# First feed-forward product of a decoder layer: both halves of the normed rows moved as one stream of 512 columns

## The reference

```python
u = rms_norm(h, norm_mix)
z = u @ w_in
h = h + concat([rwkv7_time_mix(z[..., :RWKV_IN]), moba_attention(q, k, v)]) @ w_mix_out
h = h + memory_cross_attention(rms_norm(h, norm_xattn), rms_norm(mem, norm_mem), w_xq, w_xkv, w_xo)
a = square(relu(rms_norm(h, norm_ffn) @ w_ff1))      # 1024 -> 4096
h = h + a @ w_ff2                                    # 4096 -> 1024
out = rms_norm(h, norm_final)
```

## Time and profile before

| | us |
|---|---|
| median of 3 runs | 478.35 (477.77 to 478.5) |
| profiled execution, whole | 479.23 |
| its span, first to last instruction | 477.2 |
| TensorE busy | 459.2 |
| VectorE busy | 316.0 |
| ScalarE busy | 235.7 |
| mean granted TensorE clock | 0.994 |

### The profile page before, as it was taken

How to read it: one execution, slowest core, us unless ns; L and a number is a source line. 1 busy time by engine, 2 the same in 40 slices (tenths; PEclk the granted TensorE clock), 3 DMA queues, 4 the chain that set the end, 5 groups by cost and what they waited for, 6 DMA issues and landing times.

```text
span 477.2 us, 11032 instructions
## 1 busy us (share of the span) xinstructions
PE 459.2 (96%) x4774; PEld 429.8 (90%) x4774; DVE 316.0 (66%) x459; ACT 235.7 (49%) x357; POOL 34.8 (7%) x50
## 2 busy tenths in 40 slices
PE   4999999999999999999999997999999999999994
PEld 4999999989898899999998997989898989898983
DVE  4688999897576459668656486555466555554646
ACT  5779843343354235335543453544374555453534
POOL 8100000000000000151000053000000000000000
PEclk9999999999999999999999998999999999999998
DMA  7963534505060523554452363756555555756602
GB/s 256 332 218 102 177 105 159 182 10 172 3 203 15 166 89 99 168 177 142 133 166 89 94 181 97 232 169 198 178 178 177 177 181 178 233 195 205 197 2 88
DMA packets 61411, 73.09 MB, mean 153 GB/s; under 512 B 1314, under 2 KB 51572, under 8 KB 61364
## 3 DMA queue, kind: packets, MB, share of 16 engines
q1 hardware_dynamic: 61284, 72.14, 47.3%
q0 software_dynamic: 80, 0.26, 0.1%
HBM read 71.35 MB, written 1.05 MB: 152 GB/s over the span
## 4 chain that ended last, share of the span: by engine, by line
PE 90%; DVE 5%; issue 1%; DMA 1%; ACT 1%; SPq 0%; ACTq 0%; DVEq 0%
PE bank L482 17%; PE bank L483 16%; PE bank L484 16%; PE bank L499 6%; PE bank L500 6%; PE bank L501 6%; PE bank L449 2%; PE bank L450 2%; PE bank L451 2%; PE bank L851 2%; DMA xval<-in_x 1%; PE bank L875 1%; PE bank L611 1%; DVE w_lo L1543 1%; PE bank L777 1%
## 5 line engine op out<-in xcount | busy, mean ns | idle before, releaser
L1543 DVE TENSOR_TENSOR w_lo<-raw,w_hi 128x1024 fp32r<-128x1024 f32 x130 | 160.3, 1242 | 84.2 <-ACT w_hi L1051 84.0
L1051 ACT ACTIVATE w_hi<-raw 128x1024 fp32r<-128x1024 f32 x130 | 136.6, 1057 | 140.0 <-PE bank L484 80.1
L482 PE MATMUL bank<-op_hi,w_hi 128*128 128x256 f32 x672 | 195.1, 290 | 3.8 <-DVE w_lo L1543 3.0
L483 PE MATMUL bank<-op_lo,w_hi 128*128 128x256 f32 x672 | 190.7, 284 | 0.4 <-issue 0.4
L484 PE MATMUL bank<-op_hi,w_lo 128*128 128x256 f32 x672 | 190.7, 284 | 0.0
L482 PEld LDWEIGHTS bank<-op_hi,w_hi 128*128 128x128 f32 x672 | 129.4, 192 | 6.7 <-issue 4.6
L483 PEld LDWEIGHTS bank<-op_lo,w_hi 128*128 128x128 f32 x672 | 129.5, 193 | 0.5
L484 PEld LDWEIGHTS bank<-op_hi,w_lo 128*128 128x128 f32 x672 | 129.4, 193 | 0.4 <-issue 0.4
L499 PE MATMUL bank<-w_hi,op_hi 128*128 128x512 f32 x128 | 49.9, 390 | 0.0
L500 PE MATMUL bank<-w_lo,op_hi 128*128 128x512 f32 x128 | 49.9, 390 | 0.0
L501 PE MATMUL bank<-w_hi,op_lo 128*128 128x512 f32 x128 | 49.8, 389 | 0.0
(11 more groups left out here) (247 smaller groups left out, 487.1 us busy)
## 6 DMA issues: line engine op xcount, KB each, us to landing
raw<-in_w_ff SPq DMA_DIRECT2D x32, 1024.0 KB, 5.4
raw<-in_w_in SPq DMA_DIRECT2D x12, 1024.0 KB, 5.5
raw<-in_w_xkv SPq DMA_DIRECT2D x8, 1024.0 KB, 5.7
raw<-in_w_mix_out SPq DMA_DIRECT2D x4, 1024.0 KB, 5.0
raw<-in_w_xq SPq DMA_DIRECT2D x4, 1024.0 KB, 5.1
raw<-in_w_xo SPq DMA_DIRECT2D x4, 1024.0 KB, 5.7
xval<-in_x SPq DMA_DIRECT2D x2, 512.0 KB, 4.8
raw<-in_w_in SPq DMA_DIRECT2D x2, 512.0 KB, 5.7
```

The costliest lines, as they stand in the source:

```text
L482: mm(dst, wh[:, k, :], op_hi[which][:, k, :], start=first, stop=False)
L483: mm(dst, wh[:, k, :], op_lo[which][:, k, :], start=False, stop=False)
L1051: op(view(w_hi), r, ACT.Copy).then_inc(hi_done, 1)
L1543: tt(view(w_lo), r, view(w_hi).bitcast(f32), ALU.subtract).then_inc(lo_done, 1)
```

## The change

An `f1` half now moves the hi and the lo rows at once: the two operand tiles become one tile of [128, 2, 8, 256], and a step k is one matmul of 512 columns with w_hi, whose results land side by side (hi rows in columns 0 to 255, lo rows in columns 256 to 511), and one of 256 columns with w_lo, added to the first side. So a half fills a bank; the halves take the two banks in turn. ScalarE copies the second side into `tmp` (`part`), VectorE adds the first side to it (`add`), which frees the bank, and when both halves of a unit are there it takes relu and square in one instruction (`square`). ScalarE rounds the square (`hidden`), VectorE forms the lo part. The first `f1` unit no longer has its quarters mixed with those of the second one.

```diff
-    _late = {"mix": 0, "xo": 1, "f1": 1}.get(UNITS[_u][0])
+    _late = {"mix": 0, "xo": 1}.get(UNITS[_u][0])
...
-    elif _u == len(UNITS) - 1:
+    elif _u == len(UNITS) - 1 or UNITS[_u][0] == "f1" and UNITS[_u][4] == 0:
         QUARTERS += [(2 * _u + _i, _p) for _p in range(2) for _i in range(2)]
...
-        op_hi = [sb(f"op{i}_hi", [128, KT, T], f32r) for i in range(2)]
-        op_lo = [sb(f"op{i}_lo", [128, KT, T], f32r) for i in range(2)]
+        op_both = [sb("op0", [128, 2, KT, T], f32r), None]
+        op_hi = [op_both[0][:, 0, :, :], sb("op1_hi", [128, KT, T], f32r)]
+        op_lo = [op_both[0][:, 1, :, :], sb("op1_lo", [128, KT, T], f32r)]
...
+        def half_no(s):
+            return s - OUTS[FIRST["f1"]][1] if UNITS[s // 2][4] < 2 else 2 * UNITS[s // 2][4] + s % 2
+        def half_bank(s):
+            return dense_bank[(s + 1) % 2]
... (TensorE, quarter)
+                    if what == "f1":
+                        half = half_no(s)
+                        if half < 2:
+                            pe.wait_ge(out_taken, FIRST["f1"] - 1 + half)
+                        else:
+                            pe.wait_ge(dve_add, half - 1)
...
+                if what == "f1":
+                    b = half_bank(s)
+                    for k in range(4 * part, 4 * part + 4):
+                        first, final = q == BEGUN[s] and k % 4 == 0, q == DONE[s] and k % 4 == 3
+                        if opening and k % 2 == 0:
+                            pe.wait_ge(dve_op, op_no("xo", k // 2) + 1)
+                        if final:
+                            mm(b[:, 0:T], wl[:, k, :], op_hi[0][:, k, :], start=False, stop=False)
+                        last = mm(b[:, :], wh[:, k, :], op_both[0][:, :, k, :], start=first, stop=final)
+                        if not final:
+                            mm(b[:, 0:T], wl[:, k, :], op_hi[0][:, k, :], start=False, stop=False)
+                    if q == DONE[s]:
+                        last.then_inc(dense_mm, 1)
+                    return
... (ScalarE)
+            def part(n, half):
+                s = OUTS[FIRST["f1"] + n][1] + half
+                act.wait_ge(dense_mm, s + 1)
+                if n >= 2:
+                    act.wait_ge(dve_square, n - 1)
+                op(tmp[:, n % 2, T * half:T * half + T], half_bank(s)[:, T:2 * T], ACT.Copy).then_inc(act_part, 1)
             def hidden(o):
                 n = nth(o)
-                act.wait_ge(out_taken, o + 1)
+                act.wait_ge(dve_square, n + 1)
                 k = 4 * (n // 2 % 2) + 2 * (n % 2)
-                op(op_hi[1][:, k:k + 2, :], pair(tmp[:, n % 2, :]), ACT.Square).then_inc(act_hidden, 1)
+                op(op_hi[1][:, k:k + 2, :], pair(hid_sq[:, n % 2, :]), ACT.Copy).then_inc(act_hidden, 1)
-            def take(o):
-                ...
-                op(tmp[:, n % 2, :], dense_bank[o % 2][:, :], ACT.Relu).then_inc(out_taken, 1)
... (VectorE)
+            def add(n, half):
+                s = OUTS[FIRST["f1"] + n][1] + half
+                dve.wait_ge(act_part, 2 * n + half + 1)
+                x = tmp[:, n % 2, T * half:T * half + T]
+                tt(x, half_bank(s)[:, 0:T], x, ALU.add).then_inc(dve_add, 1)
+            def square(n):
+                dve.wait_ge(dve_add, 2 * n + 2)
+                if n >= 2:
+                    dve.wait_ge(dve_hidden, n - 1)
+                x = tmp[:, n % 2, :]
+                stt(out=hid_sq[:, n % 2, :], in0=x, scalar=0.0, in1=x, op0=ALU.max, op1=ALU.mult).then_inc(dve_square, 1)
             def hidden(n):
-                dve.wait_ge(out_taken, FIRST["f1"] + n + 1)
-                sq = hid_sq[:, n % 2, :]
-                link(tt(sq, tmp[:, n % 2, :], tmp[:, n % 2, :], ALU.mult))
                 dve.wait_ge(act_hidden, n + 1)
```

More of the change, by code:

```diff
@@ L1299, in _ @@
             hi(9)
-            follow(2)
+            load(1, 0)
             rates()
-            hi(10)
             key_sums()
             follow(3)
+            hi(10)
             hi(11)
@@ L1308, in _ @@
             hi(12)
+            hi(13)
             follow(4)
-            hi(13)
-            factor()
[L1312 to L1319, removed]
+            hi(14)
+            follow(5)
+            load(1, 1)
+            hi(15)
+            hi(16)
+            follow(6)
+            hi(17)
+            factor()
             hi(18)
-            tokens()
-            vtokens()
             hi(19)
@@ L1439, in _ @@
             hi(77)
+            part(3, 0)
             hi(78)
+            rms(3)
             hi(79)
+            follow(35)
             hi(80)
+            part(3, 1)
+            part(4, 0)
+            follow(36)
             hi(81)
-            take(36)
             hi(82)
-            follow(36)
+            part(4, 1)
+            part(5, 0)
             hi(83)
             hi(84)
+            follow(37)
+            part(5, 1)
             hi(85)
-            take(37)
             hi(86)
@@ L1482, in _ @@
             hi(103)
+            part(10, 0)
             hi(104)
             hi(105)
-            residual(2)
-            residual(3)
-            take(43)
-            follow(43)
             hi(106)
+            follow(42)
+            part(10, 1)
             hi(107)
-            take(44)
-            follow(44)
             hi(108)
@@ L1495, in _ @@
             hi(110)
+            part(11, 0)
+            follow(43)
             hi(111)
+            part(11, 1)
             hi(112)
+            part(12, 0)
+            follow(44)
             hi(113)
-            take(45)
-            follow(45)
+            part(12, 1)
             hi(114)
             hi(115)
-            take(46)
-            follow(46)
             hi(116)
+            part(13, 0)
+            follow(45)
+            part(13, 1)
             hi(117)
@@ L1510, in _ @@
             hi(121)
-            take(47)
-            follow(47)
+            part(14, 0)
+            follow(46)
+            part(14, 1)
             hi(122)
             hi(123)
-            take(48)
+            hi(124)
+            residual(3)
+            hi(125)
+            part(15, 0)
+            follow(47)
+            part(15, 1)
             follow(48)
-            hi(124)
-            hi(125)
             hi(126)
@@ L1978, in _ @@
             lo(9)
-            diagonal_of(1)
-            follow(2)
             take(3)
             sums()
-            follow(3)
-            spread_copy(1)
             key_norm()
             lo(10)
-            key_root()
+            sides()
+            load(1, 0)
+            follow(3)
             lo(11)
             take(4)
+            lo(12)
+            key_root()
+            follow(4)
+            take(5)
+            lo(13)
+            lo(14)
             keys(0)
+            lo(15)
@@ L1991, in _ @@
             keys(1)
-            lo(12)
-            follow(4)
-            lo(13)
-            take(5)
-            reads(0)
-            keys(2)
-            lo(14)
-            lo(15)
             follow(5)
             take(6)
+            follow(6)
             lo(16)
+            reads(0)
+            lo(17)
+            lo(18)
+            take(7)
+            load(1, 1)
+            keys(2)
+            lo(19)
+            take(8)
+            lo(20)
+            lo(21)
+            take(9)
@@ L2187, in _ @@
             lo(95)
+            add(7, 1)
+            square(7)
+            add(8, 0)
             lo(96)
             lo(97)
-            follow(41)
+            hidden(7)
+            add(8, 1)
+            square(8)
             lo(98)
             lo(99)
-            follow(42)
             lo(100)
+            add(9, 0)
             lo(101)
@@ L2197, in _ @@
             lo(103)
+            hidden(8)
+            add(9, 1)
+            square(9)
+            add(10, 0)
             lo(104)
             lo(105)
-            follow(43)
+            hidden(9)
+            add(10, 1)
             lo(106)
             lo(107)
-            follow(44)
             lo(108)
```

430 lines of the change are left out of this document (229 added, 201 removed).

## The result

The changed kernel takes 481.0 us (median of 5 runs, 480.1 to 482.5), the kernel before on the same chip 478.5. The medians lie 2.5 us apart; the ratio, taken over all runs, is 1.0062, with a 95% interval of 1.0044 to 1.0080, which is 3.0 us: slower by 0.6%, where 2.8 us faster was forecast and the range ended at 479.6. The two profiled executions show less of the difference: that of the changed kernel took 480.11 us, the lowest of its five, and that of before 479.23, above its median. Their spans are 478.3 and 477.2, 1.1 apart.

What follows compares the result with a forecast made beforehand. TensorE, with work for 96% of the span, was taken as the bound. Stream -3.4, xo to f1 -0.9, start +0.5 and mixer +1.0 took the profiled 479.23 to 476.4 us; for the median, 478.35 - 2.8 = 475.5 us, range 472.0 to 479.6.

Steps and rivals of the forecast that it cites:

- The mixer: Mixer jobs spread anew among the dense quarters: equal TensorE work, one more wait priced, +1.0 us, bounds -1.6 and +4.
- The stream: TensorE's f1 matmuls: a step falls from 0.360 to 0.3467 us over 256 steps, -3.4 us, bounds -3.4 and 0.
- Rival 1: f1 matmuls: the wide stream saves nothing, the operand's break costing 0.0133 us per instruction; 478.9 us, chance 0.14.
- From xo to f1: Change from last xo unit to f1: 4.6 us lost before becomes 3.7 in four pieces, -0.9 us, bounds -4.6 and +1.5.
- (a): From xo to f1: lo(65) stands behind follow(30) and take(31) on VectorE, so half 65 starts 0.9 us late.
- (b): From xo to f1: half 67 waits 0.65 us for the last xo unit's bank, which take(32) frees.
- (c): From xo to f1: last two k of half 66 wait 1.55 us for follow(32), 2.7 us long beside GpSimd.
- (d): From xo to f1: half 68 waits 0.6 us for the first add, which stands behind hi(69) and its copy.
- Banks, ScalarE and VectorE: In f1: banks come free in time and the engines' added work stays beside TensorE, so it costs nothing.
- rival 2: f1 banks come free late: 18 halves each wait 0.5 us, 484 us, or 0.3 us each, 481 us; chance 0.12.
- Rival 3: The mixer's new order waits at its upper bound: +3 more than taken, 478.5 us, up to 480; chance 0.14.
- rival 4: Waits at f1 mostly vanish, all but (c), and the mixer's two with them: -7.5, 471 us; chance 0.08.

Runs made afterwards that it cites:

- experiment 1: The changed kernel with the three lists of calls of the kernel before up to values(3): 474.4 us, ratio 0.9917 to the kernel before.
- experiment 2: The kernel before, its own f1 kept, with the changed kernel's lists of calls up to values(3): 484.7 us, ratio 1.0144 to the kernel before.
- experiment 7: The kernel of experiment 1 with the f1 operand laid out so 512 columns lie in one piece: 474.2 us, ratio 0.9918 to the kernel before.
- experiment 9: The kernel of experiment 1 with lo(68) put ahead of follow(32) in VectorE's list: 477.3 us, ratio 0.9982 to the kernel before.
- experiment 4: The changed kernel with one dense quarter moved between the two parts of the second join: 478.75 us, ratio 1.0007 to the kernel before.
- experiment 5: The changed kernel with SyncE holding the load of unit 17 until the second join ends: 480.2 us, ratio 1.0038 to the kernel before.
- experiment 6: The kernel of experiment 5 with the load held until the first four outq are done: 481.7 us, ratio 1.0075 to the kernel before.

## Why the prediction was wrong, step by step

*The mixer*, "one more wait of the size of the 0.9 us one: +1.0 us", is the step that failed. Measured are +6.6 to +6.9 us (experiments 1 and 2, by medians and by ratios), 5.7 of them up to `gate` and 0.9 behind it. I followed the lists for waits on engines and found small ones. They are there, but sum to some 2.0 us, twice the price: 1.4 for lo parts and 0.6 for ScalarE. The larger part, some 4.3 us, is one that I put at nothing: stops in which TensorE has no instructions (+2.7) and the lower clock behind the longest (+1.5 to 1.7). "TensorE's work is equal; only waits can change" was my ground, and I didn't ask whether its instructions arrive, though the diff puts 128 matmuls of 12 ns in a row and the reader can see SyncE's 1 MB loads between them. "The clock" was then priced at `f1` alone, and fell here. Even the bound of +4 was too near. The stop isn't the same in every execution: 2.40 us in the profiled, fastest one of the changed kernel, 2.97 in the profiled, slowest one of experiment 2. Why it varies stays open.

*The stream*, -3.4 us, was mis-sized: the right direction, -1.9. From the start of a 512 to that of its 256 it takes some 0.235 us, not 0.2267, and from there to the next 512 0.117, not 0.120; TensorE in order of time, changed kernel:

```profile
299.85 0.39 PE L495 MATMUL bank<-op,w_hi 128*128 128x512 f32 x1
300.08 0.28 PE L497 MATMUL bank<-op,w_lo 128*128 128x256 f32 x1
300.19 0.39 PE L495 MATMUL bank<-op,w_hi 128*128 128x512 f32 x1
300.43 0.28 PE L497 MATMUL bank<-op,w_lo 128*128 128x256 f32 x1
300.54 0.39 PE L495 MATMUL bank<-op,w_hi 128*128 128x512 f32 x1
```

A run of 32 steps went from 11.52 to 338.28 - 327.01 = 11.27 us, 0.352 per step for the 0.3467 forecast: (0.360 - 0.3525) x 256 = 1.9. Each spacing had been read in a stretch of equal widths; mixed, they don't add. Rival 1 (the break costs the 0.0133 us) is out by experiment 7; its sum by the Trainium skill's 2.5 ns per matmul (TensorE: Matmul & The Clock Gate, "Wait — 56ns, not 53.3ns?"), -0.6 us, is out by the 1.9 measured.

*From xo to f1*, -0.9 us, was too little: some -2.5. This is what is left of the 4.8 us that the changed kernel gains from the first `f1` half on, less the stream's 1.9 and the 0.3 us of piece (a), which falls ahead of it. (By the starts at the place itself it is -2.1: 4.6 before, 2.5 after, each with the slower first matmul behind a wait. The 4.6 came out in the prediction with the clock at 1.6 us; the starts give 1.4 for it and 3.2 for the wait.) The mechanism was right and all four pieces were mis-sized: (a) 0.3 us for 0.9, (b) 0.94 for 0.65, (c) 0.50 for 1.55, (d) nothing for 0.6. The clock stays at 1.00. Piece (c) is short mostly because `follow(32)` takes 1.92 us here, not 2.7; VectorE in order of time, changed kernel:

```profile
285.99 3.19 DVE L1585 TENSOR_TENSOR w_lo<-raw,w_hi 128x1024 fp32r<-128x1024 f32 x2
289.11 1.91 DVE L1646 SCALAR_TENSOR_TENSOR op<-hT,par,op 128x256 fp32r<-128x256 f32 x2
...
292.07 0.68 DVE L1605 TENSOR_TENSOR hT<-bank,hT 128x512 f32<-128x512 f32 x1
293.73 1.92 DVE L1646 SCALAR_TENSOR_TENSOR op<-hT,par,op 128x256 fp32r<-128x256 f32 x2 [0.98 <-ACT op L1101]
```

Experiment 9 shows that the place of `lo(68)` alone is worth 2.9 us, the clock included. The new order of the first quarters without the wide stream wasn't tried.

*Banks, ScalarE and VectorE*, 0, held. The waits list has no entry for an `add`. The groups after, from 290 to 472 us, stand near the costs taken (0.42, 0.39, 0.745, 0.63 us):

```profile
L1655 DVE TENSOR_TENSOR tmp<-bank,tmp 128x256 f32<-128x256 f32 x32 | 13.5, 421 | 21.5 <-ACT tmp L1110 21.5
L1110 ACT ACTIVATE tmp<-bank 128x256 f32<-128x256 f32 x32 | 11.9, 373 | 20.2 <-PE bank L495 20.2
L1663 DVE SCALAR_TENSOR_TENSOR s<-tmp 128x512 f32<-128x512 f32 x16 | 11.0, 690 | 0.4
...
L1117 ACT ACTIVATE op_hi<-s 128x512 fp32r<-128x512 f32 x16 | 10.0, 623 | 3.8 <-DVE s L1663 3.8
```

So rival 2 didn't happen. That its milder case, "with 0.3 us each: 481 us", gives the very time measured is chance. *The start*, +0.5, was -0.1 (17.94 to 17.82).

*The sum* by the profiled spans: -1.9 - 2.5 - 0.1 and +5.8 for the mixer (5.95 with the earlier start put back and piece (a) taken out) make +1.3, against +1.1. It closes nearly by construction, since two terms are differences of the same starts. Rival 3, the mixer's new order, had the right place, but waits on engines as its reason and +4 us at most for 6.6, and its 0.14 was too small; rival 4's low waits at `f1` came in part together with it. All three of my own signs of being wrong came true: the mixer's waits passed 4 us (they sum to over 6), the clock fell again, and a half is slower than 2.8 us, if barely (11.27 / 4 = 2.82). That the change wins 4.0 us without the mixer's new order doesn't make the forecast right, since it was for the kernel with that order.

## What to carry to other kernels

When calls are only moved, count instructions per microsecond on the engine, not its work: a row of short matmuls needs the next block of instructions early, and a big DMA beside it makes that late. Keep such bursts apart with long-running work between them, and away from the loads. The kernel before did both: three dense quarters stand between its two parts, and 57 and 4 GB/s were on the move beside them (105.9 to 107 and 111 to 113 us), so which of the two protects it was not separated. One quarter between them left stops of 1.30 and 0.55 us beside the load (experiment 4); holding the load left 0.49 and 0.22 at the join, but only moved the long stop (5 and 6). And when a change brings a new piece of work and new lists, price and time the two apart; here one was worth 4 us and the other cost nearly 7.

## What the runs showed of the hardware

- TensorE most likely ran out of instructions: the waits show only the word "issue", and the rest is the timing of the packets and experiments 4 to 6. The instruction queue's 16 KB packet came 1.1 us after the burst began beside a 1 MB load, and 0.9 us before it without one; work went on 2.3 to 2.7 us after the packet, in nine cases.
- A stop of 2.4 to 3.3 us was followed by a granted clock under 1.00 each time (0.57 over 3.98 us in the changed kernel), and so was the wait of 2.0 us in experiment 9; stops of 0.5 to 1.4 us in the traces of experiments 4 and 5 were not.
- At 0.50 a matmul of 256 columns with new weights begins every 0.213 us, at 1.00 every 0.120: the step to the lower level costs a factor of 1.78, not 2.
- A moving operand in two runs of 256 columns, 2048 elements apart, costs nothing: 11.28 us against 11.28.
- Widths that alternate cost more than they do in stretches: 0.3525 us for 512 + 256, 0.350 with two of each together, against 0.3467 worked out from the earlier trace rows.
- Two VectorE instructions that take 0.87 us alone (in experiment 9 too, once GpSimd was done) took 1.9 us beside GpSimd here, and 2.67 before. The Trainium skill (SBUF — State Buffer, "Who interferes with whom") has them wait for each other, and the trace agrees; the size of the loss differs from order to order.
